# Two more gate tiles move from the prompt's attention into the sample attention

## The chip, the cores and the metric

One program on one core of a Trainium2 chip. The metric is the device time of one execution in microseconds; lower is better. Before the change the median of three runs is 2464.46 us (2463.84 to 2467.98).

## The reference

Two request groups go through the same two layers: a prompt of 256 rows and a sample group of 8 batches of 16 rows, each batch with 512 cached keys. The layer's middle part, cut to what matters here:

```python
def token_mixing(h, pos, past, ...):          # h: 1024 wide, 256 + 128 rows
    qkv_sb, qkv_fox, f_logit, qkv_dsa, q_idx, k_idx, w_idx, gate_logit = split(h @ w_in)
    ...
    o_sb  = stick_breaking_attention(q_sb, ks_sb, vs_sb, pos, k_pos)     # 6 heads of 64
    o_fox = forgetting_attention(q_fox, ks_fox, vs_fox, ...)
    o_dsa = dsa_attention(q_dsa, ks_dsa, vs_dsa, q_idx, w_idx, ks_idx, ...)  # over the top-k keys
    y = einsum('btnc,ncd->btnd', stack(o_sb, o_fox, o_dsa), w_branch)
    gates = sigmoid(gate_logit)               # (rows, 3 branches, 1024)
    return sum(gates * y) @ w_out
```

`gate_logit` is 3072 columns of the input projection, and nothing needs it before the attention of all three branches is done. So its matmuls can be placed anywhere between the projection and the merge. Each is a full contraction over 1024 for 384 rows.

## The kernel before

Everything is written out by hand for five engines with semaphores between them; each engine goes through its own list in the order of the code. All data is float32.

**The gate tiles.** The 3072 gate columns are 24 tiles of 128 columns, numbered 0 to 23. A tile is 8 matmuls (k = 0 to 7) of a 128x128 weight against H (128 x 384) into one PSUM bank; the profile counts each of these matmuls twice, so a tile is 16 entries of L972 (or of L1119), a half is 8. ScalarE then copies the bank out (`take_gate`, L1416) and adds to `gate_taken`. Three tiles share one weight load of 1.5 MB in two DMAs (`gates(g)`, g = 1 to 7, holds tiles 3g to 3g + 2), which SyncE issues into a ring of two slots once the tile that used the slot last is done (`gate_ready`). Tables say where each tile stands: `GATE_FIRST`, `GATE_INDEX`, `GATE_SCORE`, `GATE_PROMPT`, `GATE_FIRST_UNIT`, `GATE_UNIT`.

**The prompt's attention** is six iterations `it` (branch `it // 2`, query half `it % 2`). TensorE in an iteration waits for `p_done` of that iteration (VectorE has made the probabilities), turns them (L1064, 12 matmuls), issues the scores two iterations ahead (`prompt_scores`, L1029), multiplies by the values (L1074), and then runs the gate tiles of `GATE_PROMPT[it + 1]`. `GATE_PROMPT[0]` stands before iteration 0. VectorE in an iteration first scales and biases the scores of the next one (`biased`, L2205 and L2209), then makes this iteration's probabilities: in the stick-breaking branch by six scans (L2032) and two multiplications (L2233), whose end is `p_done`.

**The sample attention** is 18 units of four groups (a group is two heads of one batch), six units to a branch, in one step each. TensorE's step s is:

```python
def step(s):
    ...                            # scores of unit s, L1168; each step begins here
    if s >= 2: output(s - 2)       # L1128, waits ou_ready of output_rows(s - 2) on VectorE
    if s >= 1: turn_probs(s - 1)   # L1139
    if s + 2 < NSTEP: turn_three(s + 2)    # L1094, turns cached keys, waits for their DMA
    if s >= 1: turn_new_probs(s - 1)       # L1145, waits o_free of VectorE
    if s in GATE_UNIT: gate_half(*GATE_UNIT[s])    # L1119, four of a tile's eight matmuls
    if s >= 1: values(s - 1)       # L1159, waits for VectorE's copy L2271
    if s + 2 < NSTEP: turn_fourth(s + 2)
```

VectorE's step scales the scores (L2301), copies the output (L2263) and the turned probabilities (L2269, L2271), then in the first branch scans and multiplies (L2032, L2319), then finds a part of the top 128 keys of the third branch (`choose_some`: `ROUND_S[s]` rounds of L2286 and L2289, 17 rounds in all, `WKS` in RING), and last weighs the rows of unit s - 1 (`output_rows`, L2277 or L2280). After the last rounds, in step 9, the mask is stored to memory by SyncE (L582), and GpSimd loads it back in pieces as the bias of the units 12 to 17 (L1708), in one queue with the cached values (L1684).

**SyncE** loads the cached keys of a batch (L568, 768 KB) into one of three buffers, as soon as the buffer's last group is turned; for unit u that is in step u - 2. Between two of these loads stands `gates(7)`. The loop over s there runs from -2, and its part s waits for the turns of step s.

Of the kernel before, what the change touches and what calls it, by code (L numbers as in the profile page):

```python
# [60 lines left out]
GATE_FIRST = [0, 1, 2]  # L61
GATE_INDEX = [3, 4, 5]
GATE_SCORE = [6, 7]
GATE_PROMPT = [[8, 9, 10], [11, 12], [13], [14], [15], [16]]
GATE_FIRST_UNIT = 17
GATE_UNIT = {u: (18 + i // 2, i % 2) for i, u in enumerate((0, 1, 2, 4, 5, 7, 9, 11, 13, 15, 17, 18))}
ROUND_P = {0: 2, 2: 3, 3: 3}
ROUND_S = {0: 1, 1: 2, 2: 2, 3: 1, 4: 2, 5: 2, 6: 1, 7: 2, 8: 2, 9: 2}


N_IN, N_OUT, N_PROJ, N_GATE, N_BRANCH, N_WOUT = 11, 8, 10, 8, 4, 2
# [59 lines left out]
def last_unit(n):  # L131

    return divmod(NPAIR * n + NPAIR - 1, UNIT)
# [3 lines left out]
def program(nc, t):  # L137
    with ExitStack() as ctx:
# [227 lines left out]
        def _(sp):  # L366
# [126 lines left out]
            for l in range(DEPTH):  # L493
# [45 lines left out]
                def gates(g):  # L539
                    r = R_GATE + g - 1  # L540
                    if g <= 2:
                        sp.wait_ge(p2_ready, l * SEVEN_PROJ + SEVEN_PROJ - 2 + g)
                    else:
                        sp.wait_ge(gate_ready, l * 24 + 3 * (g - 1))
                    load(l, r, by_k(l, r, w, COL_GATE + g * MIX, MIX))
# [14 lines left out]
                def load_keys(n):  # L560

                    r, b = divmod(n, NB)
                    ck = t[("cache_sb_k", "cache_fox_k", "cache_dsa_k")[r]]
                    if n >= KBUF:
                        u, i = last_unit(n - KBUF)
                        sp.wait_ge(kt_ready, 2 * (l * NSTEP + u) + 1 + i // 3)
                        settle(sp)
                    sp.dma_start(KC[:, n % KBUF, :, :],  # L568
                                 ck[l, b].rearrange("(c p) h d -> p c (h d)", p=P)).then_inc(k_full[n % KBUF], 16)
# [4 lines left out]
                for s in range(-2, NSTEP):  # L574
                    for n in range(KBUF, NCACHE):
                        if last_unit(n - KBUF)[0] == s + 2:
                            load_keys(n)
                    if s == 3:
                        gates(7)
                    if s == max(ROUND_S):  # L580
                        sp.wait_ge(msk_ready, l * 3 + 3)
                        sp.dma_start(m_s, WKS).then_inc(msk_stored, 16)  # L582
# [23 lines left out]
        def _(pe):  # L606
# [245 lines left out]
            for l in range(DEPTH):  # L852
# [110 lines left out]
                def gate_tile(n, bank, taken):  # L963

                    r = R_GATE + n // 3 - 1
                    if n % 3 == 0:
                        full(l, r)
                    if taken:
                        pe.wait_ge(gate_taken, l * 24 + taken)
                    w = ring(l, r, KD, MIX)  # L970
                    for k in range(KD):
                        mm = pe.matmul(PS[:, bank, 0:T], w[:, k, (n % 3) * P:(n % 3 + 1) * P], H[:, k, :],  # L972
                                       start=(k == 0), stop=(k == KD - 1))
                    mm.then_inc(gate_ready, 1)
# [48 lines left out]
                def prompt_scores(it):  # L1023
                    r, qt = it // 2, it % 2
                    if it:
                        pe.wait_ge(z_taken, l * 6 + it)
                    for h in range(NH):
                        s = slice(64 * (h % 2), 64 * (h % 2) + 64)
                        mm = pe.matmul(PS[:, 2 * (h % 2) + h // 4, (h // 2 % 2) * 256:(h // 2 % 2) * 256 + 256],  # L1029
                                       QKT[s, r, 0, h // 2, qt * P:(qt + 1) * P], QKT[s, r, 1, h // 2, :],  # L1030
                                       start=True, stop=True)
                    mm.then_inc(s_ready, 1)
# [16 lines left out]
                pe.wait_ge(relu_ready, l * 6 + 5)  # L1049
                gate_tile(GATE_PROMPT[0][0], 4, 0)  # L1050
                prompt_scores(1)
                pe.wait_ge(relu_ready, l * 6 + 6)
                for i, n in enumerate(GATE_PROMPT[0][1:]):
                    gate_tile(n, 4 + i, (n, 0)[i])
                pe.wait_ge(gate_taken, l * 24 + GATE_PROMPT[0][-1] + 1)
                for it in range(6):
# [22 lines left out]
                    if it == 4:  # L1079
                        pe.wait_ge(gate_taken, l * 24 + GATE_PROMPT[4][0] + 1)  # L1080
                    if it + 1 < 6:
                        for i, n in enumerate(GATE_PROMPT[it + 1]):
                            gate_tile(n, 4 + i, GATE_PROMPT[it][-1] + 1)
                        if len(GATE_PROMPT[it + 1]) > 1:
# [19 lines left out]
                def turn_fourth(s):  # L1104

                    if s >= 2:
                        pe.wait_ge(kt_free, 3 * (l * NSTEP + s) + 2)
                    turn_group(s, 3, 3 if s < 2 else 0).then_inc(kt_ready, 1)
# [33 lines left out]
                def turn_new_probs(s):  # L1142

                    pe.wait_ge(o_free, l * NSTEP + s + 1)
                    pe.transpose(PS[0:NT, 7, 2 * P:3 * P], ES[s % 2][:, PAST:KEYS], IDENT[:, :]).then_inc(st_ready, 1)  # L1145
# [17 lines left out]
                def step(s):  # L1163
# [13 lines left out]
                    if s >= 1:  # L1177
                        turn_new_probs(s - 1)
                    if s in GATE_UNIT:
                        gate_half(*GATE_UNIT[s])  # L1180
                    if s >= 1:
# [5 lines left out]
                turn_fourth(0)  # L1187
                gate_tile(GATE_FIRST_UNIT, 4, GATE_FIRST_UNIT)
                turn_three(1)
                turn_fourth(1)  # L1190
                pe.wait_ge(gate_taken, l * 24 + GATE_FIRST_UNIT + 1)
                for s in range(NSTEP):
# [3 lines left out]
                turn_new_probs(NSTEP - 1)  # L1196
                gate_half(*GATE_UNIT[NSTEP])
                values(NSTEP - 1)
# [66 lines left out]
        def _(act):  # L1265
# [119 lines left out]
            for l in range(DEPTH):  # L1385
# [217 lines left out]
                def step(s):  # L1603
# [13 lines left out]
                    if s < NU and s + 2 < NSTEP:  # L1617
                        turned_three(s + 2)
                    if s in GATE_UNIT and GATE_UNIT[s][1]:
                        take_gate(GATE_UNIT[s][0], 3)  # L1620

                act.wait_ge(po_copied, l * 6 + 6)
                turned_three(0)
                turned_fourth(0)
                take_gate(GATE_FIRST_UNIT, 4)
                turned_three(1)
                for s in range(NSTEP):
                    step(s)
                take_gate(GATE_UNIT[NSTEP][0], 3)
                act.wait_ge(gate_taken, l * 24 + 24)  # L1630
# [105 lines left out]
        def _(dve):  # L1736
# [322 lines left out]
            for l in range(DEPTH):  # L2059
# [231 lines left out]
                def step(s):  # L2291
# [24 lines left out]
                    if r == SB:  # L2316
                        dve.wait_ge(es_ready, l * NSTEP + s + 1)
                        link(reverse_product(ZS[:, 0:KEYS - 1], LS[:, 1:KEYS], ZERO[:, 1:KEYS]))
                        V.tensor_tensor(e[:, 0:KEYS - 1], e[:, 0:KEYS - 1], ZS[:, 0:KEYS - 1], ALU.mult).then_inc(ps_ready, 1)  # L2319
                    if s in ROUND_S:  # L2320
                        choose_some(sum(n for i, n in ROUND_S.items() if i < s), ROUND_S[s])
                    if s == max(ROUND_S):
                        V.tensor_scalar(WKS, WKS, TAKEN / 2, NEG, ALU.is_gt, ALU.mult).then_inc(msk_ready, 1)
# [82 lines left out]
```

## Time and profile before

| | |
|---|---|
| median of the runs | 2464.46 us |
| the profiled execution, its own time | 2463.8 us |
| its span | 2462.0 us |
| prompt attention, layer 0, gate tile 9 to the first key turn | 607.6 to 679.7 us |
| sample attention, layer 0, to the first branch projection | 679.7 to 830.3 us |
| the same two in layer 1 | 1818.0 to 1890.1, 1890.1 to 2040.1 us |
| TensorE's mean granted clock | 0.993 of full |

The profile is of one execution; times are microseconds from the start of the span. The two layers run almost the same list 1210.4 us apart, so what is read in layer 0 counts twice unless a row of layer 1 says otherwise. In a timeline row the number in brackets is the time for which the engine sat idle just before, and behind the arrow is what ended it. A row joins neighbouring instructions of one kind.

### The profile page before, as it was taken

To read this page: it belongs to the slowest core of one execution; us is meant where nothing else is said; L and a number is where in the kernel's file an instruction comes from. 1 tells how busy PE (TensorE), PEld (TensorE's weight loads), DVE (VectorE), ACT (ScalarE), POOL (GpSimd) and SP (SyncE) were. 2 spreads that over 40 slices of the span, in tenths; PEclk is the share of its full clock that TensorE was granted. 3 is DMA by queue.
4 is the path that set the end of the run, shared out by engine and by line. 5 is a ranking of instruction groups with operands and counts; after the bars stand their busy time and mean duration, and the time that the engine had idled before them with its cause. 6 is when DMAs were issued, how large, how long until landed. Compare 5 with 4: busy or idle time off the path is not lost.

```text
span 2462.0 us, 41376 instructions
## 1 busy us (share of the span) xinstructions
PE 2378.9 (97%) x17120; PEld 2049.1 (83%) x17120; DVE 1213.7 (49%) x2576; ACT 565.4 (23%) x1304; POOL 154.6 (6%) x292
## 2 busy tenths in 40 slices
PE   7999999999999999999999999999999899999998
PEld 6999996885666589999989999878656565999998
DVE  3566432533665425565255663335265844366742
ACT  3000022114544322001130000211235431410011
POOL 0000000000037100000000000000000560000000
PEclk8999999999999999999999999999999999999999
DMA  8355233762379442442424543448424993323232
GB/s 319 105 185 182 95 128 134 240 221 95 116 258 313 152 150 103 172 165 94 136 103 172 184 138 108 145 149 260 164 93 158 295 299 118 112 73 134 95 116 73
DMA packets 299915, 390.84 MB, mean 159 GB/s; under 512 B 33773, under 2 KB 245609, under 8 KB 299730
## 3 DMA queue, kind: packets, MB, share of 16 engines
q1 hardware_dynamic: 275746, 333.91, 40.6%
q0 software_dynamic: 16896, 45.43, 5.6%
q10 hardware_dynamic: 7088, 8.87, 1.0%
q8 instruction: 136, 2.23, 0.4%
q14 instruction: 49, 0.40, 0.0%
HBM read 378.54 MB, written 9.62 MB: 158 GB/s over the span
## 4 chain that ended last, share of the span: by engine, by line
PE 86%; DMA 5%; ACT 3%; DVE 2%; SPq 1%; POOL 1%; issue 1%; ACTq 0%; DVEq 0%; POOLq 0%
PE PS L719 28%; PE PS L766 12%; PE PS L972 6%; PE PS L1209 4%; PE PS L920 4%; PE PS L866 3%; PE PS L702 3%; PE PS L646 3%; PE PS L686 2%; DMA QKT<-cache_fox_k 2%; PE PS L822 2%; PE PS L942 2%; PE PS L814 2%; PE PS L1231 2%; PE PS L1223 2%
## 5 line engine op out<-in xcount | busy, mean ns | idle before, releaser
L719 PE MATMUL PS<-OT,RING 128*128 128x192 f32 x1216 | 222.5, 326 | 0.0
L719 PE MATMUL PS<-H,RING 128*128 128x192 f32 x1216 | 211.7, 327 | 0.0
L719 PE MATMUL PS<-OT,QR 128*128 128x192 f32 x1216 | 210.0, 326 | 0.0
L719 PEld LDWEIGHTS PS<-OT,RING 128*128 128x128 f32 x1216 | 201.8, 190 | 0.0
L719 PEld LDWEIGHTS PS<-H,RING 128*128 128x128 f32 x1216 | 198.0, 190 | 3.5 <-issue 3.2
L719 PEld LDWEIGHTS PS<-OT,QR 128*128 128x128 f32 x1216 | 199.7, 190 | 0.0
L972 PE MATMUL PS<-H,RING 128*128 128x384 f32 x480 | 160.9, 490 | 0.0
L1337 ACT ACTIVATE QR<-QR 128x384 f32<-128x384 f32 x76 | 39.8, 524 | 509.2 <-DVE QR L1905 509.2
L972 PEld LDWEIGHTS PS<-H,RING 128*128 128x128 f32 x480 | 89.1, 190 | 61.4 <-issue 4.7
L1684 POOL DMA_DIRECT2D QR<-cache_sb_v x16 | 12.9, 805 | 1737.2 <-DVE QR L2233 1661.4
L719 PE MATMUL PS<-H,QR 128*128 128x192 f32 x608 | 111.2, 326 | 0.0
L719 PEld LDWEIGHTS PS<-H,QR 128*128 128x128 f32 x608 | 100.9, 190 | 0.0
L1905 DVE TENSOR_TENSOR QR<-PS,QR 128x384 f32<-128x384 f32 x76 | 42.4, 557 | 109.5 <-PE PS L719 109.5
L1209 PE MATMUL PS<-OT,RING 128*128 128x384 f32 x288 | 93.4, 487 | 0.8 <-DVE OT L2263 0.8
L866 PE MATMUL PS<-RING,H 128*128 128x384 f32 (+1 forms) x288 | 90.9, 472 | 0.0
L766 PE MATMUL PS<-BIG,RING 128*128 128x192 f32 x528 | 89.7, 326 | 0.0
L1094 PE MATMUL PS<-IDENT,QKT 128*128 128x128 f32 x576 | 78.4, 279 | 10.0 <-DMA QKT<-cache_fox_k 7.0
L1209 PEld LDWEIGHTS PS<-OT,RING 128*128 128x128 f32 x288 | 54.6, 190 | 38.7 <-DVE OT L2263 1.0
L766 PEld LDWEIGHTS PS<-BIG,RING 128*128 128x128 f32 x528 | 86.5, 190 | 0.0
L1955 DVE TENSOR_TENSOR QR<-RING 128x768 f32<-128x768 f32 (+1 forms) x24 | 21.4, 890 | 125.5 <-DMA RING<-ffn_w_out 125.5
L1900 DVE TENSOR_TENSOR QR<-PS,QR 128x384 f32<-128x384 f32 x76 | 42.2, 556 | 79.5 <-PE PS L719 79.5
L1094 PEld LDWEIGHTS PS<-IDENT,QKT 128*128 128x128 f32 x576 | 63.8, 142 | 20.7 <-DMA QKT<-cache_fox_k 8.0
(309 smaller groups left out, 4238.8 us busy)
## 6 DMA issues: line engine op xcount, KB each, us to landing
RING<-ffn_w_in SPq DMA_DIRECT2D x80, 1024.0 KB, 7.2
RING<-w_in SPq DMA_DIRECT2D x64, 768.0 KB, 6.3
QR<-w_ada SPq DMA_DIRECT2D x34, 1024.0 KB, 9.7
BIG<-w_ada SPq DMA_DIRECT2D x34, 1024.0 KB, 10.5
RING<-ffn_w_out SPq DMA_DIRECT2D x32, 768.0 KB, 4.6
RING<-ffn_w_out SPq DMA_DIRECT2D x32, 640.0 KB, 5.3
QR<-cache_sb_v POOLq DMA_DIRECT2D x16, 768.0 KB, 6.5
QKT<-cache_sb_k SPq DMA_DIRECT2D x16, 768.0 KB, 4.7
```

The source lines that it names most:

```text
L646: mm = pe.matmul(PS[32 * j:32 * j + 32, bank, col:col + P], CT[:, k, :], w[:, k, j * P:(j + 1) * P], start=(k == 0), stop=(k == KD - 1))
L686: pe.matmul(PS[:, 2 * p + part, 0:HALF], w[:, k, part * 256 + jj * P:part * 256 + (jj + 1) * P], H[:, k, GROUP[0]], start=(k == 0), stop=( ...
L702: mm = pe.matmul(PS[:, 2 * p + part, GROUP[1]], w[:, k, part * 256 + jj * P:part * 256 + (jj + 1) * P], H[:, k, GROUP[1]], start=(k == 0), ...
L719: mm = pe.matmul(PS[:, bank, GROUP[g]], a[:, k, :], x[:, k, :], start=(k == 0), stop=(k == 3))
L766: mm = pe.matmul(PS[:, bank, 0:HALF], a[:, k, :], x[:, k, :], start=(half == 0 and k == 0), stop=(half == 1 and k == kn - 1))
L814: mm = pe.matmul(PS[:, m, 0:HALF], w[:, k, m * P:(m + 1) * P], HID[:, half * k2 + k, GROUP[0]], start=(half == 0 and k == 0), stop=(half = ...
L822: mm = pe.matmul(PS[:, m + 2, 0:HALF], w[:, k, m * P:(m + 1) * P], HID[:, half * k2 + k, GROUP[1]], start=(half == 0 and k == 0), stop=(ha ...
L866: mm = pe.matmul(PS[:, n % 3, 0:width], H[:, k, tt * P:(tt + 1) * P], w[:, k, :], start=(k == 0), stop=(k == KD - 1))
L920: mm = pe.matmul(PS[:, bank, GROUP[half]], a[:, k, :], x[:, k, :], start=(k == 0), stop=(k == 3))
L972: mm = pe.matmul(PS[:, bank, 0:T], w[:, k, (n % 3) * P:(n % 3 + 1) * P], H[:, k, :], start=(k == 0), stop=(k == KD - 1))
L1094: mm = pe.transpose(PS[:, bank, c * P:(c + 1) * P], KC[:, n % KBUF, c, a * P:(a + 1) * P], IDENT[:, :])
L1209: mm = pe.matmul(PS[:, n, 0:T], w[:, 3 * n + k, m * P:(m + 1) * P], OT[:, 3 * n + k, :], start=(k == 0), stop=(k == NPAIR - 1))
```

## The change

The numbers of the tables change, and one number in SyncE's list. Tiles 10 and 12 are no longer in the prompt's attention as second tiles of their places: `GATE_PROMPT` holds one tile in each place after the first, which holds two. The tile before unit 0 is number 15 and not 17. Eight tiles and not six are cut into halves: halves now stand in the steps 0 to 5, 7, 8, 9, 11, 12, 13, 15, 16 and 17 and behind the last step. New are those in the steps 3, 8, 12 and 16. The rounds of the key choice are spread anew: steps 0 and 3 have one more, steps 6 and 9 one less. `gates(7)` is issued in part 4 of SyncE's loop and not in part 3.

```diff
-GATE_PROMPT = [[8, 9, 10], [11, 12], [13], [14], [15], [16]]
-GATE_FIRST_UNIT = 17
-GATE_UNIT = {u: (18 + i // 2, i % 2) for i, u in enumerate((0, 1, 2, 4, 5, 7, 9, 11, 13, 15, 17, 18))}
+GATE_PROMPT = [[8, 9], [10], [11], [12], [13], [14]]
+GATE_FIRST_UNIT = 15
+GATE_UNIT = {u: (16 + i // 2, i % 2) for i, u in enumerate((0, 1, 2, 3, 4, 5, 7, 8, 9, 11, 12, 13, 15, 16, 17, 18))}
 ROUND_P = {0: 2, 2: 3, 3: 3}
-ROUND_S = {0: 1, 1: 2, 2: 2, 3: 1, 4: 2, 5: 2, 6: 1, 7: 2, 8: 2, 9: 2}
+ROUND_S = {0: 2, 1: 2, 2: 2, 3: 2, 4: 2, 5: 2, 7: 2, 8: 2, 9: 1}
...
-                    if s == 3:
+                    if s == 4:
                         gates(7)
```

TensorE, prompt's attention, between the values of iteration 0 (before) and the turned probabilities of iteration 1 (L1064); a minus is a row of before only:

```order
 L972 MATMUL PS<-H,RING 128x384 [waits gate_taken]
 L972 MATMUL PS<-H,RING 128x384 x7
-L972 MATMUL PS<-H,RING 128x384 [waits gate_taken,slot_full1]
-L972 MATMUL PS<-H,RING 128x384 x7
-L1064 MATMUL PS<-IDENT,QR 128x128 [waits ppt_copied,p_probs_ready,gate_taken]
+L1064 MATMUL PS<-IDENT,QR 128x128 [waits ppt_copied,p_probs_ready]
 L1064 MATMUL PS<-IDENT,QR 128x128 x3
 L1064 MATMUL PS<-IDENT,QR 128x128 [waits ppt_copied]
```

The second gate tile of the place is gone, and with it the wait for its copy; the same is taken away ahead of iteration 0.

VectorE, sample attention of layer 0, end of step 0 and start of step 1 (L2301 is the first instruction of step 1):

```order
 L2286 MAX ST<-RING 128x8
 L2289 MATCH_REPLACE RING<-ST,RING 128x528
+L2286 MAX ST<-RING 128x8
+L2289 MATCH_REPLACE RING<-ST,RING 128x528
 L353 ISA
 L2301 SCALAR_TENSOR_TENSOR DMB<-PS,ZERO 128x528
```

A second round of the key choice now stands ahead of the scores of unit 1.

SyncE, the DMAs of the sample attention of layer 0 (`w_in` is the weights of gate tiles, x2 is one `gates`):

```order
 L388 DMA RING<-w_in 128x4x384 x2
 L568 DMA QKT<-cache_sb_k 128x4x384 x5
-L568 DMA QKT<-cache_fox_k 128x4x384 x3
+L568 DMA QKT<-cache_fox_k 128x4x384 x4
 L388 DMA RING<-w_in 128x4x384 x2
-L568 DMA QKT<-cache_fox_k 128x4x384 x5
+L568 DMA QKT<-cache_fox_k 128x4x384 x4
 L568 DMA QKT<-cache_dsa_k 128x4x384 x3
 L582 DMA scr_mask_sample<-RING 128x528
```

The keys number 11 (the fourth of `cache_fox_k`) are now issued ahead of the last gate weights.

## Rows read from the trace of the kernel before

**Rows 1.** The page: the span, and busy time by engine.

```profile
span 2462.0 us, 41376 instructions
...
PE 2378.9 (97%) x17120; PEld 2049.1 (83%) x17120; DVE 1213.7 (49%) x2576; ACT 565.4 (23%) x1304; POOL 154.6 (6%) x292
```

**Rows 2.** Timeline of PE, prompt's attention, layer 0: start, us, what, [idle before].

```profile
607.60 10.59 PE L972 MATMUL PS<-H,RING 128*128 128x384 f32 x32
618.77 1.09 PE L1064 MATMUL PS<-IDENT,QR 128*128 128x128 f32 x8 [0.58 <-ACT BIG L1416]
...
623.71 10.59 PE L972 MATMUL PS<-H,RING 128*128 128x384 f32 x32
634.88 1.09 PE L1064 MATMUL PS<-IDENT,QR 128*128 128x128 f32 x8 [0.58 <-ACT BIG L1416]
```

**Rows 3.** Timeline of DVE in the same stretch.

```profile
615.86 1.94 DVE L2233 TENSOR_TENSOR QR<-QR 128x765 f32<-128x765 f32 x2
...
622.31 1.95 DVE L2205 SCALAR_TENSOR_TENSOR QR<-PS,QR 128x768 f32<-128x768 f32 x2 [2.54 <-PE PS L1029]
...
630.73 1.95 DVE L2233 TENSOR_TENSOR QR<-QR 128x765 f32<-128x765 f32 x2
```

**Rows 4.** Timeline of PE, sample attention, layer 0, steps 2 to 6.

```profile
704.40 0.41 PE L1128 MATMUL PS<-OWN,NORM 128*128 128x64 f32 x2 [0.88 <-DVE NORM L2277]
...
711.13 1.10 PE L1168 MATMUL PS<-QR,QBLK 128*32 128x264 f32 x16
...
715.07 1.30 PE L1159 MATMUL PS<-QR,NORM 128*32 128x128 f32 x33 [0.46 <-DVE NORM L2271]
...
717.02 1.10 PE L1168 MATMUL PS<-QR,QBLK 128*32 128x264 f32 x16
718.73 0.41 PE L1128 MATMUL PS<-OWN,NORM 128*128 128x64 f32 x2 [0.61 <-DVE NORM L2277]
...
725.46 1.10 PE L1168 MATMUL PS<-QR,QBLK 128*32 128x264 f32 x16
...
733.40 1.10 PE L1168 MATMUL PS<-QR,QBLK 128*32 128x264 f32 x16
```

**Rows 5.** Timeline of DVE, layer 0, step 1.

```profile
696.60 0.71 DVE L2301 SCALAR_TENSOR_TENSOR DMB<-PS,ZERO 128x528 f32<-128x528 f32 x1 [0.26 <-DVE RING L2289]
...
702.41 0.71 DVE L2286 MAX8 ST<-RING 128x8 f32<-128x528 f32 x1
...
703.96 0.29 DVE L2277 TENSOR_TENSOR NORM<-PS,OWN 128x128 f32<-128x128 f32 x1
```

**Rows 6.** Timeline of PE, waits for cached keys, steps 6 and 8 of both layers.

```profile
737.58 1.09 PE L1094 MATMUL PS<-IDENT,QKT 128*128 128x128 f32 x8 [1.69 <-DMA QKT<-cache_fox_k]
...
753.50 0.66 PE L1094 MATMUL PS<-IDENT,QKT 128*128 128x128 f32 x4 [1.63 <-DMA QKT<-cache_fox_k]
...
1947.36 1.09 PE L1094 MATMUL PS<-IDENT,QKT 128*128 128x128 f32 x8 [1.04 <-DMA QKT<-cache_fox_k]
...
1964.30 0.66 PE L1094 MATMUL PS<-IDENT,QKT 128*128 128x128 f32 x4 [2.65 <-DMA QKT<-cache_fox_k]
```

**Rows 7.** The chain that ended last: the keys of step 6, issue and us to landing.

```profile
720.98 16.55 DMA QKT<-cache_fox_k
```

**Rows 8.** Timeline of SP's queue: the last gate weights of layer 0.

```profile
717.60 1.05 SPq L388 DMA_DIRECT2D RING<-w_in  x2
```

**Rows 9.** Windows: busy time of PE, PEld, DVE, ACT, POOL, then PEclk, DMA share, GB/s.

```profile
752.00:762.00 10.00, 8.04 (x77) 5.36 (x78) 6.12 (x16) 2.91 (x5) 5.12 (x11) 0.66 1.06 311
1961.00:1970.00 9.00, 5.88 (x71) 3.31 (x69) 5.32 (x14) 2.91 (x5) 5.14 (x10) 0.81 1.07 300
```

**Rows 10.** Timeline of DVE, layer 0, step 15.

```profile
805.59 0.71 DVE L2301 SCALAR_TENSOR_TENSOR DMB<-PS,MASKS 128x528 f32<-128x528 f32 x1 [3.21 <-DMA MASKS<-scr_mask_sample]
```

**Rows 11.** Timeline of PE, layer 0, steps 15 and 16: the waits for VectorE.

```profile
807.08 0.28 PE L1145 MATMUL PS<-IDENT,QR 128*16 128x128 f32 x1 [1.58 <-DVE OT L2263]
...
815.05 1.43 PE L1159 MATMUL PS<-QR,NORM 128*32 128x128 f32 x40 [0.59 <-DVE NORM L2271]
```

## The prediction

> **What bounds the kernel now.** I read the page first, then the timeline of TensorE through both attentions, and for each idle time in it the timeline of the engine named behind the arrow. TensorE is busy for 97% of the span and VectorE for 49% [rows 1]; so time is won only where TensorE waits, and a gate tile that is moved is worth what it no longer adds in the old place less what it adds in the new one. In the prompt's attention the reader sees no large wait: the gate tiles fill it, and what ends the small waits ahead of iterations 0 and 1 is ScalarE's copy of the last gate tile [rows 2]. The question there is how late VectorE's probabilities are, which these tiles hide. In the sample attention TensorE waits in four ways: for VectorE's copies and rows of the unit before [rows 4], for cached keys [rows 6], for the mask as bias of the third branch [rows 10, 11], and twice it runs at a lower clock just behind such a wait [rows 9].
>
> **Prompt, tile 10 gone ahead of iteration 0.** Tiles 9 and 10 take 10.59 us, 5.3 each, from 607.60, and the turned probabilities start at 618.77 [rows 2]. Without tile 10 TensorE is through at 612.9. But `p_done` of iteration 0 is the end of the multiplication that began at 615.86 and took 1.94, so 617.80 [rows 3]; nothing that VectorE or ScalarE did for it waited on tile 10. With the 0.14 us that TensorE takes to start behind another engine, iteration 0 begins at 617.94: 0.83 us earlier, and TensorE stands idle for 5.0 us.
>
> **Prompt, tile 12 gone ahead of iteration 1.** The place is 623.71 to 634.30, iteration 1 begins at 634.88 [rows 2]. VectorE starts on the scores of iteration 2 at 622.31, when TensorE has issued them, and ends `p_done` of iteration 1 at 630.73 + 1.94 = 632.67, 10.36 us later and without a break [rows 3]. All of this comes 0.83 earlier: scores at 621.48, `p_done` at 631.84, iteration 1 at 631.98 in place of 634.88. That is 2.90 us in all for 11.9 us of removed tiles and copies, and a second idle time, from 628.2 to 632.0, 3.7 us. Behind it the iterations have one gate tile as before. Two layers: **-5.8 us**.
>
> **The clock in these two gaps.** TensorE's granted clock fell after an idle time of 1.63 us in layer 0 and of 2.65 in layer 1 [rows 6]: mean 0.66 over 10 us and 0.81 over 9 us [rows 9]. With 1.2 GHz in place of 2.4 as the only other level that is 6.8 and 3.4 us at half speed, so up to 3.4 and 1.7 us lost. It did not fall after 1.69 us [rows 6] nor after 1.58 [rows 11]. Gaps of 5.0 and 3.7 us do not occur in the prompt's attention now. Bounds for each: 0 and 3.4 us. I take 1.5, near the lower fall, since part of a slow stretch lies in the gap itself: four gaps, **+6.0 us**. The Trainium skill, "TensorE: Matmul & The Clock Gate", section "Why this matters for your kernels", advises against idle gaps between bursts of matmuls, because idle time takes the array back to half rate. By that rule the four gaps each cost a fall, and the sum is the one here; by the two falls and two non-falls of the trace it would be 3 us lower.
>
> **Sample, the added round in step 0.** VectorE was the late one here: it began the scores of unit 1 right behind its own round (0.26 us, released by L2289), and at the end of step 1 TensorE waited 0.88 us for `output_rows(0)` [rows 4, 5]. A round costs 703.96 - 702.41 = 1.55 us [rows 5]. It stands ahead of everything in that chain, so TensorE comes to step 2's output 1.5 later. Two layers: **+3.0 us**.
>
> **Sample, the half in step 3.** Without a half the step takes 717.02 - 711.13 = 5.89 us, step 5 with one 733.40 - 725.46 = 7.94 [rows 4]. The half is 2.6 us, of which 0.46 falls into the wait for the copy L2271 [rows 4], and 0.1 into starting: 2.05 more. Step 4 gets back its 0.61 wait for `output_rows(2)`, less 0.1, as the added round of step 3 ends just in time behind the longer step: 8.44 becomes 7.94. Net 1.55, two layers: **+3.1 us**.
>
> **Sample, steps 6 to 8 and the weights behind the keys.** Up to here the sample attention is 3.05 us late. The keys for step 6 took 16.55 us to land behind the gate weights issued at 717.60 [rows 7, 8]; now they go ahead, and the wait in step 6 (1.69 and 1.04) should vanish. But the DMA engines are full (share 1.06) [rows 9], the same bytes have to come before the third group of keys in step 8, and their stream starts 3 us later, so these land 3 us later too: what step 6 gives back, step 8 waits for. Bounds: both waits gone, and the falls of the clock behind them, 3.3 + 3.7 + 5.1 = 12.1 us less; or no step 6 gain with the delay in full, 2.7 more. I take **0**, nearer the second, since the share stays over 1. The Trainium skill, "DMA: Bandwidth & Descriptors", section "Issuing engines are not separate DMA queues", has all queues interleave on the same 16 engines. By that rule another order in one queue takes no bytes from the total, which is the 0; a reading by SyncE's queue alone would give the 12 us.
>
> **Sample, the half in step 8** stands behind the wait for keys, so it doesn't fill that; it hides the copy's wait as in step 3: 2.05, two layers **+4.1 us**. The round taken from step 6 and the one from step 9 are worth nothing: VectorE had ended before TensorE asked, and the mask's store stands in SyncE's list behind a key load that TensorE releases.
>
> **Sample, the half in step 12** is hidden. In step 15 VectorE waited 3.21 us for its bias until 805.59, TensorE then 1.58 us for VectorE [rows 10, 11]. That bias comes at the end of a chain on GpSimd that runs from the mask's store without waiting for TensorE. The 2.05 us added in step 12 fills the 1.58 and the small waits of step 13. **0**; if that chain were not the limit, +4.1.
>
> **Sample, the half in step 16** fills 0.59 of 2.6 us [rows 11], and about 0.1 of starting: **+3.8 us**.
>
> **Sum:** -5.8 + 6.0 + 3.0 + 3.1 + 0 + 4.1 + 0 + 3.8 = +14.2 us. On the profiled execution's own time of 2463.8 that is 2478.0; the median of the runs is 0.7 above that execution, so **2478.5 us**.
>
> **Rivals.**
> - *The clock stays up in the prompt's gaps.* For it: two of the four waits of this size had no fall. Against: these are at least 1 us longer than any of them. 6 us less: 2472.5. Chance 0.15.
> - *The keys come in time.* The weights behind the keys free steps 6 and 8, and with them the clock. For it: 16.55 us to landing behind 1.5 MB. Against: the full engines. 12.1 us less: 2466.4. Chance 0.13.
> - *The prompt gives its tiles back in full (the other side).* If `p_done` were not the limit, the rows ahead of iterations 0 and 1, which name ScalarE's copy, would be the whole story, and two tiles would save 11.9 us a layer without gaps: -23.8 in place of +0.2, so 2454.5. The change is faster from the point where the prompt gives over 14 us in two layers. Against: `p_done` ends at 617.80, only 0.97 before TensorE starts. Chance 0.05.
> - *The new halves cost in full.* Step 8's half runs at the low clock behind a longer wait for keys (2.6 us more in each layer), and step 12's isn't hidden (4.1): +9.3, 2488. Chance 0.12.
> - My forecast, 2474 to 2483: chance 0.50. The rest is small mixtures of these.
>
> **The numbers.** A change under 0.2% (4.9 us) can't be told from none here. Faster by more needs the third rival or an unforeseen gain: 0.06. Within: the second rival, 2466.4: 0.14. Slower: 0.80. The range leaves out the last two rivals and takes in the first two: 2466 to 2485.
>
> **What the profile of the changed kernel would show.** Right: PE idle 5.0 us (L1064, released by DVE L2233) ahead of iteration 0 and 3.7 ahead of iteration 1, both layers, the first key turn 2.9 us earlier before any loss to the clock, and PEclk under 1 near the gaps; in step 2 a wait of 2.4 for L2277; no wait for keys in step 6, one of 2 us or more in step 8; step 3 at 7.9; step 15 still waiting for L2263. I am wrong if the prompt's attention shrinks by 10 us a layer, if step 8 waits under 1 us, or if the clock stays at 1.00 from 607 to 650.

## The result and the profile after

The changed kernel takes 2482.04 us (median of 6 runs, 2481.05 to 2484.71), the kernel before 2464.15 in 6 runs beside them (2462.6 to 2467.98). The ratio is 1.0073, 95% interval 1.0063 to 1.0084: 17.9 us slower. The forecast was 2478.5, 14.0 above the median of 2464.46 that it started from.

The profiled execution of the changed kernel took 2484.45 us, 2.4 above its median, with a span of 2482.7; beside [rows 1] that is 20.7 us more. First the page: the span and the busy time by engine.

```profile
span 2482.7 us, 41374 instructions
...
PE 2389.7 (96%) x17120; PEld 2059.8 (83%) x17120; DVE 1214.7 (49%) x2576; ACT 563.6 (23%) x1304; POOL 153.9 (6%) x292
```

TensorE has the same 17120 entries as before and is busy for 10.8 us more; VectorE, ScalarE and GpSimd have the same work. The same matmuls took longer; the windows further down show the lower clock that does it. The other half of the 20.7 us (9.9) is idle time. The timeline of TensorE in the prompt's attention of layer 0, which answers to [rows 2]:

```profile
608.18 5.43 PE L972 MATMUL PS<-H,RING 128*128 128x384 f32 x16
618.53 2.89 PE L1064 MATMUL PS<-IDENT,QR 128*128 128x128 f32 x12 [4.92 <-DVE QR L2233]
...
624.57 5.43 PE L972 MATMUL PS<-H,RING 128*128 128x384 f32 x16
633.60 2.92 PE L1064 MATMUL PS<-IDENT,QR 128*128 128x128 f32 x12 [3.60 <-DVE QR L2233]
```

One gate tile stands in each place now, and behind it TensorE is idle for 4.92 and 3.60 us, ended by the probabilities L2233. Then the slow clock: 12 turns take 2.9 us, where 8 of them took 1.09 before [rows 2]. In the next view, windows with the columns of [rows 9], the first two are the prompt's attention of both layers and the last two the sample attention.

```profile
606.69:680.51 73.82, 62.15 (x374) 42.12 (x373) 48.52 (x71) 39.18 (x89) 1.68 (x2) 0.93 0.34 112
1823.97:1898.70 74.73, 63.06 (x373) 42.65 (x373) 48.54 (x71) 39.20 (x89) 1.57 (x2) 0.91 0.33 110
680.51:838.07 157.56, 145.23 (x1567) 97.33 (x1567) 87.51 (x209) 64.60 (x104) 75.24 (x142) 0.98 0.83 266
1898.70:2058.63 159.93, 146.82 (x1567) 98.15 (x1567) 87.22 (x209) 64.59 (x104) 75.26 (x142) 0.97 0.82 263
```

And the same view of the kernel before, over its prompt attention (end of gate tile 8 to the first key turn):

```profile
606.11:679.69 73.58, 68.77 (x406) 45.21 (x405) 48.54 (x71) 40.01 (x91) 1.68 (x2) 1.00 0.36 118
```

The prompt's attention of each layer gave up 16 of its matmuls, 32 entries, and takes 73.82 and 74.73 us in place of 73.58 and 73.57, with a granted clock of 0.93 and 0.91 in place of 1.00. In the sample attention the first place to look at is step 2. The timeline of TensorE of the changed kernel, answering to the first of [rows 4], and then the waits for keys of steps 7 and 8 in both layers, answering to [rows 6]:

```profile
706.77 0.41 PE L1128 MATMUL PS<-OWN,NORM 128*128 128x64 f32 x2 [2.41 <-DVE NORM L2277]
707.02 0.94 PE L1139 MATMUL PS<-IDENT,QR 128*128 128x128 f32 x4
707.75 2.77 PE L1094 MATMUL PS<-IDENT,QKT 128*128 128x128 f32 x12
...
754.05 0.63 PE L1094 MATMUL PS<-IDENT,QKT 128*128 128x128 f32 x4 [1.78 <-DMA QKT<-cache_fox_k]
...
760.54 0.66 PE L1094 MATMUL PS<-IDENT,QKT 128*128 128x128 f32 x4 [1.53 <-DMA QKT<-cache_fox_k]
...
1967.53 2.79 PE L1094 MATMUL PS<-IDENT,QKT 128*128 128x128 f32 x12 [2.65 <-DMA QKT<-cache_fox_k]
```

The wait for `output_rows(0)` has gone from 0.88 to 2.41, as the added round says, but behind it the 12 key turns take 2.77 us in place of 1.47. There is no key wait in step 6. The keys are waited for in steps 7 and 8 in layer 0 (1.78 and 1.53 us), and in layer 1 in step 7 (2.65), with slow turns behind it; layer 1's step 8 waits only 0.25. Last, the timeline at the mask, answering to [rows 11]: the wait for the copy L2263 in step 12 (in the kernel before it is as long, 1.23, and the half is new behind it), the start of step 15's turned rows, and step 16 with its half and no wait.

```profile
791.53 0.28 PE L1145 MATMUL PS<-IDENT,QR 128*16 128x128 f32 x1 [1.23 <-DVE OT L2263]
791.65 2.81 PE L1119 MATMUL PS<-H,RING 128*128 128x384 f32 x8
...
812.91 0.27 PE L1145 MATMUL PS<-IDENT,QR 128*16 128x128 f32 x1
813.02 2.75 PE L1119 MATMUL PS<-H,RING 128*128 128x384 f32 x8
815.69 1.30 PE L1159 MATMUL PS<-QR,NORM 128*32 128x128 f32 x33
```

A step is the distance between the first score matmuls (L1168) of neighbouring steps. Read so from TensorE's timelines, in us, layer 0 and layer 1:

| | before | after | difference, two layers | forecast |
|---|---|---|---|---|
| start to the prompt's attention | 606.11 | 606.69 | +0.6 | 0 |
| prompt's attention | 73.58, 73.57 | 73.82, 74.73 | +1.4 | +0.2 |
| step 2 | 8.71, 8.71 | 11.90, 11.91 | +6.4 | +3.0 |
| steps 3 to 5 | 22.27, 22.27 | 23.82, 23.66 | +2.9 | +3.1 |
| steps 6 to 9 | 34.04, 32.94 | 34.56, 35.54 | +3.1 | +4.1 |
| steps 12 to 15 | 30.85, 31.32 | 30.56, 32.10 | +0.5 | 0 |
| step 16 | 4.59, 4.60 | 6.52, 6.52 | +3.9 | +3.8 |
| the rest, most of it behind layer 1's attention | | | +1.9 | 0 |
| span | 2462.0 | 2482.7 | +20.7 | +14.2 |

The first difference and that of the rest are not shown to belong to the change: over the fourteen traces, with the same code there, the start to the prompt's attention takes 603.8 to 608.5 us, the stretch between the two layers' attentions 985.2 to 987.9 and what is behind the second 421.9 to 422.4, but 424.1 in the changed kernel and 424.0 in `w_early`.

### The profile page after: what moved, and what is told of

Read it like the earlier page. It is cut to its first block, busy times and chain, and to the rows that moved or that the text cites. A ratio compares the mean times of both kernels' runs of the same rounds, so it can differ in the third digit from the quotient of the medians.

```text
span 2482.7 us, 41374 instructions
## 1 busy us (share of the span) xinstructions
PE 2389.7 (96%) x17120; PEld 2059.8 (83%) x17120; DVE 1214.7 (49%) x2576; ACT 563.6 (23%) x1304; POOL 153.9 (6%) x292
## 4 chain that ended last, share of the span: by engine, by line
PE 88%; DMA 4%; DVE 3%; ACT 3%; issue 1%; SPq 1%; POOL 0%; ACTq 0%; DVEq 0%; POOLq 0%
PE PS L719 28%; PE PS L766 12%; PE PS L972 5%; PE PS L920 4%; PE PS L1209 4%; PE PS L866 3%; PE PS L646 3%; PE PS L702 3%; PE PS L942 2%; PE PS L1119 2%; PE PS L686 2%; PE PS L822 2%; PE PS L814 2%; PE PS L1094 2%; PE PS L1231 2%; PE PS L1223 2%
## 5 line engine op out<-in xcount | busy, mean ns | idle before, releaser
L719 PEld LDWEIGHTS PS<-H,RING 128*128 128x128 f32 x1216 | 198.0, 190 | 3.5 <-issue 3.2
L972 PE MATMUL PS<-H,RING 128*128 128x384 f32 x416 | 140.3, 491 | 0.0
L972 PEld LDWEIGHTS PS<-H,RING 128*128 128x128 f32 x416 | 76.9, 190 | 53.0 <-issue 4.7
L1905 DVE TENSOR_TENSOR QR<-PS,QR 128x384 f32<-128x384 f32 x76 | 42.3, 557 | 109.6 <-PE PS L719 109.6
L1119 PE MATMUL PS<-H,RING 128*128 128x384 f32 x256 | 90.0, 495 | 0.0
```

Source lines behind the costliest of these rows:

```text
L719: mm = pe.matmul(PS[:, bank, GROUP[g]], a[:, k, :], x[:, k, :], start=(k == 0), stop=(k == 3))
L1119: mm = pe.matmul(PS[:, 3, 0:T], w[:, k, (n % 3) * P:(n % 3 + 1) * P], H[:, k, :], start=(k == 0), stop=(k == KD - 1))
```

## The experiments

Each kernel was timed in five rounds beside the kernel before, whose medians in the four batches were 2463.7 to 2464.8; the ratio is to that kernel, with its 95% interval. Steps are named as above. The intervals of `r0_undo`, `w_early`, `h12_cut`, `fill_p` and, by a hair, `w_cut` overlap that of the changed kernel, so there the difference of two medians is a rough figure and the argument stands on the step times of the traces, one execution each.

**1 and 2. Less work in the prompt's attention alone** (kernel before). `p_cut` leaves out seven of the eight matmuls of tiles 10 and 12, `p_fit` only two and four of them.

```diff
-                    for k in range(KD):
+                    last = {10: 1, 12: 1}.get(n, KD)      # p_fit: {10: 6, 12: 4}
+                    for k in range(last):
...
-                                       start=(k == 0), stop=(k == KD - 1))
+                                       start=(k == 0), stop=(k == last - 1))
```

> The kernel before, with seven of the eight matmuls of gate tiles 10 and 12 left out (their results are not the full product); nothing is moved, the sample attention is untouched. The prompt's part of the change by itself. My theory (TensorE then waits for p_done, 5.0 and 3.7 us, and its clock falls behind both gaps): the prompt's attention gets 0 to 1.5 us longer in each layer in spite of 9.3 us less matmul work, so 2463 to 2467 us. Rival, the clock costs nothing: 5.8 us less, 2458.5. Rival, the gates were the limit: 18 us less or more, 2446.

> The kernel before, with only two of the eight matmuls of tile 10 and four of those of tile 12 left out, so that about 1.0 us of idle time stays ahead of iterations 0 and 1. My theory: p_done sets the start of both iterations just as in p_cut, but the clock stays up, so the full 5.8 us come off: 2458.5 us, with more matmul work than p_cut and less time. Rival (a gap costs by its own length or by work behind it, not by the clock): as p_cut.

Measured: `p_cut` 2467.27 us (2462.09 to 2469.18), ratio 1.0013 [1.0004, 1.0022]; `p_fit` 2455.86 (2455.34 to 2456.85), 0.9968 [0.9957, 0.9979]. The timeline of TensorE of `p_cut` and then of `p_fit`, layer 0, ahead of iterations 0 and 1 (`p_cut`'s file is one line longer, so L1064 is L1065 there):

```profile
620.30 2.89 PE L1065 MATMUL PS<-IDENT,QR 128*128 128x128 f32 x12 [4.27 <-DVE QR L2234]
...
623.12 1.81 PE L1030 MATMUL PS<-QKT 64*128 64x256 f32 x12
...
635.45 1.06 PE L1065 MATMUL PS<-IDENT,QR 128*128 128x128 f32 x8 [3.00 <-issue]
```

```profile
617.98 1.06 PE L1065 MATMUL PS<-IDENT,QR 128*128 128x128 f32 x8 [1.05 <-DVE QR L2234]
619.29 0.66 PE L1065 MATMUL PS<-IDENT,QR 128*128 128x128 f32 x4 [0.25 <-ACT QR L1581]
619.88 1.57 PE L1030 MATMUL PS<-QKT 64*128 64x256 f32 x12
...
631.95 1.06 PE L1065 MATMUL PS<-IDENT,QR 128*128 128x128 f32 x8 [1.06 <-ACT BIG L1417]
```

The wait of 4.27 us has slow turns behind it (2.89 for 12), that of 1.05 has not. Against the expectation the second wait of `p_cut`, 3.00 us ahead of iteration 1, has none either, in both layers: the fall came behind one of its two gaps. With the clock up, in `p_fit`, the prompt's attention takes 70.59 and 70.60 us, 3.0 less than before in each layer, which is the term of -5.8. In `p_cut` it takes 71.77 and 71.83, although that runs eight matmuls less than `p_fit` in each layer: 1.2 us is the price of the one fall. So the removed work beyond some six matmuls buys nothing, and the wait in its place costs.

`p_fit` is also 2.6 us below its expected 2458.5. In its trace the clock stays up behind the waits for keys too (2.24 us in layer 0's step 8, 1.75 in layer 1's), where the kernel before has its two falls [rows 9]; that the cut brings this about isn't shown. Of the 11.4 us between the medians of `p_cut` and `p_fit` the prompt's attention explains 2.4. Their profiled executions are 6.7 us apart, and most of the rest lies where neither edit reaches: 2.3 us ahead of the first attention and 2.6 between the layers.

**3 and 4. The round in step 0, added alone and taken back alone.** `r0_add` is the kernel before, `r0_undo` the changed kernel; the round goes from step 6 to step 0 and back.

```diff
 r0_add
-ROUND_S = {0: 1, 1: 2, 2: 2, 3: 1, 4: 2, 5: 2, 6: 1, 7: 2, 8: 2, 9: 2}
+ROUND_S = {0: 2, 1: 2, 2: 2, 3: 1, 4: 2, 5: 2, 7: 2, 8: 2, 9: 2}
 r0_undo
-ROUND_S = {0: 2, 1: 2, 2: 2, 3: 2, 4: 2, 5: 2, 7: 2, 8: 2, 9: 1}
+ROUND_S = {0: 1, 1: 2, 2: 2, 3: 2, 4: 2, 5: 2, 6: 1, 7: 2, 8: 2, 9: 1}
```

> The kernel before with one of the rounds of the key choice moved from step 6 to step 0, nothing else. My theory: TensorE waits 2.4 in place of 0.9 us in step 2 (1.5 us in each layer, 3.0) and its clock falls behind that wait as in the changed kernel (1.7 in each layer, 3.4): 2470.5 us. Without the fall: 2467.2. Rival, the delay is taken back by the waits for keys in steps 6 and 8: 2464.

> The changed kernel with step 0's added round taken back and given to step 6. My theory: 6.4 us less than the changed kernel's 2482.0, 2475.6 us, and no fall of the clock in step 2. Rival, the keys are the limit up to step 8, so that an earlier TensorE only waits longer for them: 2480 to 2482.

Measured: `r0_add` 2469.78 us (2467.35 to 2472.28), 1.0029 [1.0017, 1.0040], so +6.1 beside the kernel before (2463.7); step 2 takes 11.90 and 11.89. The round costs 3.2 us in each layer's step 2, twice its own 1.5. `r0_undo` 2478.82 (2471.41 to 2479.38), 1.0056 [1.0042, 1.0069]: 3.2 less than the changed kernel, not 6.4, which lies between the theory and the rival. Step 2 is back at 8.71 and 8.70, so the 6.4 are won there. The timeline of `r0_undo` on TensorE, step 2 and then steps 7 and 8, shows where they go:

```profile
703.33 0.41 PE L1128 MATMUL PS<-OWN,NORM 128*128 128x64 f32 x2 [0.88 <-DVE NORM L2277]
...
743.64 1.50 PE L1094 MATMUL PS<-IDENT,QKT 128*128 128x128 f32 x12 [1.83 <-DMA QKT<-cache_fox_k]
...
755.93 0.66 PE L1094 MATMUL PS<-IDENT,QKT 128*128 128x128 f32 x4 [2.62 <-DMA QKT<-cache_fox_k]
```

Steps 7 and 8 together take 22.99 and 24.46 us in place of 20.89 and 21.87: 4.7 us given back, by longer waits for keys and by the slow clock behind them. Here a gain ahead of step 7 was worth half or less.

**5 and 6. The keys.** `w_early` is the changed kernel with `gates(7)` issued one part earlier, as before. `w_cut` keeps the order and issues a quarter of those bytes.

```diff
 w_early
-                    if s == 4:
+                    if s == 3:
                         gates(7)
 w_cut
+                    if few:
+                        parts = [(dst[:, 0:1, :], src[:, 0:1, :]) for dst, src in parts]
...
-                        gates(7)
+                        gates(7, few=True)
```

> The changed kernel with the last gate weights issued one part earlier in SyncE's loop, ahead of the keys number 11 as before the change; they now wait there for the half in step 3. My theory (the DMA engines are full, so another order in the queue moves a wait and saves nothing): 2480 to 2484 us, with a wait for keys in step 6 again and less of it in steps 7 and 8. Rival, the order matters: several us to one side.

> The changed kernel, with three quarters of the bytes of the last gate weights left out: `gates(7)` loads one k slice of each four (2 x 192 KB in place of 2 x 768 KB), so that tiles 21 to 23 are multiplied with what an earlier load left in the slot for the other slices; the instructions of all engines stay. It asks why the keys of the steps 7 and 8 come late. My theory of the 0 term (the DMA engines are full, share 1.06, and what counts is the bytes in all): 1.15 MB less at the 330 GB/s of this stretch is 3.5 us of transfer, as much as the longest wait of layer 0 and more than the 2.65 of layer 1; the waits in the steps 7 and 8 go or shrink to under 0.5 us, and so do the falls of the clock behind them. The four steps 6 to 9 then cost 5.9, 7.9, 7.9 and 7.8, so 29.5 in place of 34.6 and 35.5 us: 11 us less in two layers, 2471. Rival (the keys' own stream sets it: each load starts only when TensorE has turned the batch before, and takes its time whatever else moves): the waits stay within 0.5 us, 2480 to 2483. If the engines that fetch the values on GpSimd's queue use the room instead, something between, 2475 to 2478.

Measured: `w_early` 2478.89 us (2476.24 to 2483.81), 1.0063 [1.0049, 1.0077], an interval that overlaps that of the changed kernel. Steps 6 to 8 take 10.09, 9.13, 7.79 in layer 0, a wait for keys of 2.44 us being back in step 6; their sums are 27.01 and 26.67 against 26.78 and 27.76 after. The order of the weights and keys moves the wait and hardly the sum.

`w_cut` took 2476.3 (2475.35 to 2477.66), 1.0052 [1.0038, 1.0065], 5.7 less than the changed kernel. First the transfers from issue to landing (x, KB each, median us), layer 0 from 715 to 760 us, in the changed kernel and then in `w_cut`:

```profile
QKT<-cache_fox_k SPq DMA_DIRECT2D x7, 768.0 KB, 11.5
QR<-cache_fox_v POOLq DMA_DIRECT2D x5, 768.0 KB, 8.8
```

```profile
QKT<-cache_fox_k SPq DMA_DIRECT2D x7, 768.0 KB, 8.6
QR<-cache_fox_v POOLq DMA_DIRECT2D x5, 768.0 KB, 7.9
```

Then TensorE's waits of `w_cut` from 730 to 840 us (us in total, times, the longest):

```profile
PE PS L1148 <- DVE OT L2266: 2.9, 4, 1.3
PE PS L1131 <- DVE NORM L2283: 1.5, 2, 0.8
PE PS L1162 <- DVE NORM L2274: 1.4, 3, 0.5
PE PS L1097 <- DMA QKT<-cache_dsa_k: 0.9, 1, 0.9
```

No wait for `cache_fox_k` is left in either layer, steps 7 and 8 take 7.88 and 7.93 in layer 0, and steps 6 to 9 sum to 29.48 and 29.72 against 34.56 and 35.54: 10.9 us less, the 11 of the theory. That the keys are late because of the weights' bytes beside them is thereby shown, and the rival that their own stream sets the time is out. By which way the bytes delay them the run can't tell from the keys alone, since keys and weights stand in SyncE's one queue; but the cached values in GpSimd's queue landed a little sooner too (8.8 and then 7.9 us). Steps 10 to 15 take 46.41 and 48.63 in place of 44.09 and 45.63: TensorE now runs into the third branch's keys in step 11 (0.9 us in layer 0) and waits longer for the mask, in layer 0's step 15 and in layer 1's step 12 (3.08). 5.3 of the 10.9 us are given back there; the 2471 expected had not counted that.

**7 and 8. The new halves.** `h12_cut` and `h3816_cut` are the changed kernel and leave out three of four matmuls of the half in step 12, and of those in steps 3, 8 and 16.

```diff
-                    for k in range(4 * half, 4 * half + 4):
+                    for k in ((7 * half,) if cut else range(4 * half, 4 * half + 4)):
...
-                        gate_half(*GATE_UNIT[s])
+                        gate_half(*GATE_UNIT[s], cut=s in (12,))      # h3816_cut: (3, 8, 16)
```

> The changed kernel with three of the four matmuls of the half in step 12 left out. My theory: this half is hidden behind the chain of mask and bias on GpSimd, so nothing comes off: 2481 to 2483 us, and step 15 waits about 1.6 us for L2263 again. Rival, the half costs in full: 3.9 us less, 2478.

> The changed kernel with three of the four matmuls of the halves in steps 3, 8 and 16 left out, 1.97 us each. My theory: steps 8 and 16 give 1.4 to 1.5 us each in each layer; step 3 gives nothing, because with two rounds in it VectorE's output_rows(2) ends at the same time and TensorE waits for it in step 4. Together 5.8 us less, 2476.2. Rival, every half costs the same: 9 us less, 2473.

Measured: `h12_cut` 2480.61 us (2479.73 to 2481.2), 1.0071 [1.0057, 1.0085]: 1.4 less than the changed kernel, with overlapping intervals. Steps 12 to 15 take 30.81 and 32.41 without most of the half, 30.56 and 32.10 with it. The expected wait for L2263 in step 15 came back in layer 1 alone (1.42 us). In layer 0 TensorE comes 0.7 us earlier to the wait in step 12, which ends no sooner (1.91 for 1.23), and the clock falls behind it to a mean of 0.62 over 3 us. So taking the half away saves nothing, but part of that is this fall, and `b_1712` below is the cleaner evidence. `h3816_cut` 2473.73 (2472.26 to 2476.27), 1.0045 [1.0031, 1.0058]: 8.3 less, which is nearer the rival's 9 than my 5.8. It isn't the sum of three halves, though. Step 3 falls to 5.85 and 5.99, but the row of its step 4 on TensorE is this:

```profile
724.27 0.41 PE L1128 MATMUL PS<-OWN,NORM 128*128 128x64 f32 x2 [2.04 <-DVE NORM L2277]
724.51 1.02 PE L1139 MATMUL PS<-IDENT,QR 128*128 128x128 f32 x4
```

The second round of step 3 is late now, and behind a wait of 2.04 us four turned probabilities take 1.02 in place of 0.61: step 4 takes 11.54. The steps 3 and 4 sum to 17.4, more than the 15.9 with the half. Half and round in step 3 belong together. Steps 7 and 8 take 13.74 us in both layers in place of 20.89 and 21.87: without the half, and also without any wait for keys, for which TensorE now comes later. Of these 15.3 us steps 9 to 15 give back 10.0; in step 11 the third branch's keys are waited for 2.69 and 1.71 us. Step 16 takes 4.6, so 3.8 less in two layers. The price of the half in step 8 can't be read off this run by itself.

**9 and 10. Matmuls that nobody reads.** `fill_p` is the changed kernel with six and four matmuls into a free bank in the two gaps of the prompt's attention; `fill_p2` has these and three more in the wait of step 2.

```diff
+                def filler(m):
+                    for _ in range(m):
+                        pe.matmul(PS[:, 5, 0:T], IDENT[:, :], H[:, 0, :], start=True, stop=True)
+
+                filler(6)                 # ahead of iteration 0; filler(4) ahead of iteration 1
...
+                    if s == 2:            # fill_p2 alone
+                        pe.wait_ge(st_copied, l * NSTEP + 1)
+                        for _ in range(3):
+                            pe.matmul(PS[:, 6, 0:T], IDENT[:, :], H[:, 0, :], start=True, stop=True)
```

> The changed kernel with extra matmuls whose result nobody reads in the two idle times of the prompt's attention: six of the shape of a gate matmul (3.96 us) ahead of iteration 0, four (2.64 us) ahead of iteration 1. All of the computation is done, and 6.6 us of work is added in each layer. My theory, the clock is what the gaps cost: no fall in the prompt's attention, which goes from 73.8 and 74.7 us to 70.7 in each layer, so 7 us less than the changed kernel's 2482.0: 2475. Rival, the gaps cost only their own length: 2482, or more if the added work gets in the way.

> As fill_p, and three more unread matmuls (1.97 us) in step 2 of the sample attention, where TensorE waits 2.4 us for VectorE. My theory: the fall of the clock behind that wait goes too and step 2 goes from 11.9 to 10.2 us, 3.4 in two layers: 2471.5. Rival, given back by the waits for keys in steps 7 and 8, as half of r0_undo's gain was: 2473 to 2475.

Measured: `fill_p` 2478.45 us (2474.67 to 2480.37), 1.0058 [1.0045, 1.0072], 3.6 less than the changed kernel where 7 was expected; `fill_p2` 2473.46 (2471.52 to 2475.89), 1.0038 [1.0024, 1.0051], 8.6 less, an interval clear of the changed kernel's. The timeline of TensorE in `fill_p2`, in the prompt's gap (L1057 are the unread matmuls) and in step 2 (L1181):

```profile
606.20 5.43 PE L972 MATMUL PS<-H,RING 128*128 128x384 f32 x16
611.47 4.03 PE L1057 MATMUL PS<-H,IDENT 128*128 128x384 f32 x12
616.55 1.06 PE L1069 MATMUL PS<-IDENT,QR 128*128 128x128 f32 x8 [1.05 <-DVE QR L2244]
...
699.09 2.20 PE L1181 MATMUL PS<-H,IDENT 128*128 128x384 f32 x6
701.56 0.41 PE L1135 MATMUL PS<-OWN,NORM 128*128 128x64 f32 x2 [0.27 <-DVE NORM L2288]
701.80 0.60 PE L1146 MATMUL PS<-IDENT,QR 128*128 128x128 f32 x4
702.25 1.47 PE L1101 MATMUL PS<-IDENT,QKT 128*128 128x128 f32 x12
```

The wait ends by the same instruction of VectorE, but what follows runs at full clock: 12 key turns in 1.47 us and not 2.77. The prompt's attention takes 70.58 to 70.59 us in both kernels, 3.2 and 4.1 less than in the changed kernel, and step 2 in `fill_p2` 10.23 and 10.24, 1.67 less each. These are prices of the clock alone, since no work went away: 7.4 us for the prompt's two gaps in two layers (7.1 by the mean of the six traced kernels with both gaps, 3.0 to 4.2 in each layer) and 3.3 for step 2. The sum 10.7 would give 2471.3. As in `r0_undo` the keys take part of it back: steps 7 and 8 together take 23.60 and 22.74 us in `fill_p2`, and the sample attention of `fill_p` takes 2.4 us more in both layers together than that of the changed kernel.

**11 and 12. Halves placed by the waits** (kernel before). `b_1712` moves the half of step 17 to step 12. `b_best` also moves that of step 9 to step 6, with a round from step 9 to step 6.

```diff
 b_1712
-... enumerate((0, 1, 2, 4, 5, 7, 9, 11, 13, 15, 17, 18))}
+... enumerate((0, 1, 2, 4, 5, 7, 9, 11, 12, 13, 15, 18))}
 b_best
-... enumerate((0, 1, 2, 4, 5, 7, 9, 11, 13, 15, 17, 18))}
+... enumerate((0, 1, 2, 4, 5, 6, 7, 11, 12, 13, 15, 18))}
-ROUND_S = {0: 1, 1: 2, 2: 2, 3: 1, 4: 2, 5: 2, 6: 1, 7: 2, 8: 2, 9: 2}
+ROUND_S = {0: 1, 1: 2, 2: 2, 3: 1, 4: 2, 5: 2, 6: 2, 7: 2, 8: 2, 9: 1}
```

> The kernel before with one gate half moved from step 17 to step 12 (steps 0, 1, 2, 4, 5, 7, 9, 11, 12, 13, 15 and behind the last), nothing else: all of the computation is done. My theory: the half costs nothing in step 12 and 1.9 us in step 17, so 3.8 us less: 2460.3. Rival, a half costs the same wherever it stands: 2464.

> The kernel before with two halves moved: 17 to 12 as in b_1712, and 9 to 6, with the rounds of the key choice moved along (step 6 two, step 9 one). All of the computation is done. My theory: the half in step 6 lies in the stretch whose end the keys of step 8 set, so it costs about 0.5 us there and 2.05 in step 9; 3 us less than b_1712's 2459.3: 2456.3. Rival, delays in step 6 hold up the issue of the keys and come back in step 8: 2459 to 2460.

Measured: `b_1712` 2459.33 us (2457.92 to 2462.24, 11 runs), 0.9982 [0.9973, 0.9991]: 4.8 us faster than the kernel before and 22.7 faster than the changed one. Only `p_fit`, with its work left out, is below it. With a half more in them, steps 12 to 15 take 30.89 and 30.91 us in place of 30.85 and 31.32: step 12 is longer (9.58 for 7.27 in layer 0), and step 15 shorter (7.79 for 9.54). `b_best` 2462.27 (2459.37 to 2466.51), 0.9995 [0.9986, 1.0004]: no difference that can be told, outside what theory and rival had given. The steps 8 and 9 fall to 5.7 and 7.1 us, but TensorE then comes too early for what follows. The timeline of VectorE in its layer 1, step 12:

```profile
1991.16 0.71 DVE L2301 SCALAR_TENSOR_TENSOR DMB<-PS,MASKS 128x528 f32<-128x528 f32 x1 [5.19 <-DMA MASKS<-scr_mask_sample]
```

The mask is late by 5.19 us there; in layer 0 the third branch's keys cost 2.77 us in step 11.

## Why the forecast was right, and which terms were off

The direction came out, the measured median lies 1 us inside the forecast's own band of 2474 to 2483, and the terms for the prompt, step 3, step 12 and step 16 came out as priced. The terms that were off hardly cancelled: the round in step 0 and the clock in the prompt were both too small, by 3.4 and by 1.1 to 1.4 us, and the keys a little too dear. Point by point:

- **The prompt gives back 5.8 us.** Right. VectorE ends the wait, the gaps are 4.92 and 3.60 us for 5.0 and 3.7, and with the clock up the attention is 3.0 us shorter in each layer (`p_fit`, `fill_p`), 6.0 in all. The rival in which it gives its tiles back in full is out. (By [rows 2] the removed tiles and copies are 11.7 us a layer, not 11.9; only that rival's time hangs on it.)
- **The clock in the gaps, +6.0.** Right in kind, a little small: 7.4 in the traces of the changed kernel, by the unread matmuls of `fill_p`. The rule cited from the Trainium skill ("TensorE: Matmul & The Clock Gate", section "Why this matters for your kernels") had a fall behind each gap; the trace of the changed kernel agrees with that: both layers show slow turns behind both gaps (4.92 and 3.60 us). Of `p_cut`'s gaps the one of 4.27 had a fall and the one of 3.00 had none.
- **The round in step 0, +3.0.** The wait was right and the size half of what it should be: 6.4. This is the term that failed. The wait is the 2.4 us that the text names, but the step priced only the wait. The trace of before had a fall of the clock behind a wait of 1.63 [rows 6], so a fall behind a wait that grows from 0.88 to 2.41 had to be given a chance and a price, as it was in the prompt's gaps. Seven kernels have this wait with nothing in it (the changed one, `r0_add`, `w_early`, `w_cut`, `h12_cut`, `h3816_cut`, `fill_p`); in 13 of their 14 traces of step 2 it takes 11.89 to 11.92 us, in one, layer 1 of `h12_cut`, 10.23 behind the same 2.40. The difference is 1.67, the lower of the two falls in the prediction (1.7).
- **Step 3, +3.1.** Right: 2.9 for steps 3 to 5. `h3816_cut` adds that half and round have to come together.
- **Steps 6 to 8, 0, and step 8's half, +4.1.** The sum over steps 6 to 9 is +3.1. What step 6 gives back is waited for further on, as said, but in step 7 as well as in 8: layer 0's two waits are 1.78 and 1.53, and in layer 1 the wait is in step 7 (2.65) and step 8 waits 0.25. So the wait of 2 us or more in step 8 did not come, and in layer 1 the text's own sign of being wrong (under 1 us in step 8) did; the sum held although the place was missed. That bytes and not order make the waits is shown by `w_early` (other order, same sum) and `w_cut` (fewer bytes, no wait). The sentence of the Trainium skill cited there ("DMA: Bandwidth & Descriptors", "Issuing engines are not separate DMA queues") is about queues of different engines, and keys and weights share one; the values in GpSimd's queue, 8.8 us and with fewer weights 7.9, agree with it. How the +3.1 divides between the keys and the half in step 8 isn't shown.
- **Step 12, 0.** Right as a price, by `b_1712` and `h12_cut`; wrong in the sign given for it. Step 15 waits for L2263 no longer [rows 11]: 7.79 for 9.54 in layer 0. Step 12 is 2.0 longer in layer 0, as the half stands behind the wait of 1.23 and doesn't fill it; the steps 13 and 15 give it back, as TensorE now asks for the mask's later pieces after they have come.
- **Step 16, +3.8.** Right: 3.9 in the table, 3.8 back by `h3816_cut`.

What the sum left out is 6.5 us of span: 3.4 in step 2, 1.2 in the prompt, 1.9 behind the attentions, 0.6 ahead of them, 0.5 at the mask, less 1.1 at the keys and in steps 3 to 5. The 1.9 are mostly a stretch of slow clock at 2058.8 us, just behind layer 1's attention (granted clock 0.74 from 2056 to 2062); the other trace with so long an end is that of `w_early`, the other twelve traces don't have it, and what sets it was not tried. Against the median, which lies 2.4 below the profiled execution, 3.5 us are missing, about the size of the term that failed.

Open: what sets the 2.3 and 2.6 us between `p_cut` and `p_fit` outside the attentions, and what decides whether the clock falls behind a wait. Its length alone doesn't. The kernel before has a fall behind 1.63 us, while these two waits have none (timeline of TensorE of `fill_p`, step 8, and of `b_best`, layer 1, step 12):

```profile
756.06 0.66 PE L1101 MATMUL PS<-IDENT,QKT 128*128 128x128 f32 x4 [3.15 <-DMA QKT<-cache_fox_k]
```

```profile
1992.36 0.28 PE L1145 MATMUL PS<-IDENT,QR 128*16 128x128 f32 x1 [3.27 <-DVE OT L2263]
```

The granted clock is 1.00 in the 4 us behind each.

## What to carry to other kernels

Work that fills a wait can be worth more than its hidden time: when it is moved away, ask what the wait that stays would cost with a fall of the clock behind it (here 1.7 us in a layer behind a wait of 2.4, 3.0 to 4.2 behind the prompt's two gaps), and move only as much as leaves the wait near the 1.05 us that cost nothing. A trace that shows the clock up behind one wait doesn't say that it stays up behind the next. Where a chain of late data (keys, then a mask) lies ahead, a gain upstream is worth what those waits leave of it: by the medians, which are rough here, 3.2 of 6.4, 5.7 of 10.9, 8.6 of 10.7. Place movable work in a step whose later waits give it back (step 12), not in one where they don't (steps 16 and 17).

## What was not expected of the hardware

- Added matmuls made the kernel faster: 13 unread ones in each layer, at 0.67 us each (12 entries in 4.03, two to a matmul) some 17 us of TensorE's time in the two layers, took 8.6 us off the total (2482.04 to 2473.46).
- The wait of 2.4 us in step 2 was followed by a fall to 1.2 GHz in 13 cases of 14, while waits of 3.00 (`p_cut`, both layers), 3.06 (`h12_cut`), 3.15 (`fill_p`) and 3.27 us (`b_best`) elsewhere were followed by none. The prompt's waits of 1.02 to 1.06 us in `p_fit`, `fill_p` and `fill_p2` never were.
- A key load of 768 KB lands 11.5 us behind its issue while the last gate weights move beside it, and 8.6 with three quarters of them gone (medians of 7); in both the DMA engines' share is 1.05 to 1.06 from 744 to 764 us, so the share doesn't show whether keys will be late.
